# Prompt attention of branch A as one causal softmax per head, with branch counts in its bias table

## The reference

```python
# A: 8 heads of 64, branches (window, dilation) = (128,1), (512,4), (2048,16)
for window, dil in A_PATTERNS:      # keys i, i-dil, ..., i-window: up to 129 of them
    o, lse = banded_attn(qa, ka, va, rel_bias[:, :8], dil, window // dil, None)
oa = merge_branches(outs, lses)     # softmax over the three lse, weighted sum
# B: 8 query heads, 2 kv heads, window 128, a learned sink in each head's denominator
ob, _ = banded_attn(qb, kb, vb, rel_bias[:, 8:], 1, 128, sinks)
mixed = concat([oa, ob]); out = mixed @ w_out
```

## Time and profile before

| | |
|---|---|
| time of three runs, median (lowest to highest) | 2607.88 us (2606.56 to 2607.96) |
| the profiled execution | 2608.48 us, span 2606.7 us |
| TensorE busy | 90% |
| VectorE, ScalarE, GpSimd busy | 34%, 21%, 31% |
| granted TensorE clock, mean | 0.94 of full |
| prompt attention | 1264 to 1628 us |

### The profile page before, as it was taken

How to read it: one execution, slowest core, us unless ns; L and a number is a source line. 1 busy time by engine, 2 the same in 40 slices (tenths; PEclk the granted TensorE clock), 3 DMA queues, 4 the chain that set the end, 5 groups by cost and what they waited for, 6 DMA issues and landing times. The chain is left out here.

```text
span 2606.7 us, 37370 instructions
## 1 busy us (share of the span) xinstructions
PE 2350.6 (90%) x14418; PEld 2206.2 (85%) x14418; DVE 894.7 (34%) x2053; ACT 539.1 (21%) x781; POOL 810.4 (31%) x536
## 2 busy tenths in 40 slices
PE   4699999999999879995898776887999999999996
PEld 2599999999999779972677665876999999999995
DVE  0422222222222560024356776139222222222225
ACT  2111111111111212211233333122211111111114
POOL 1422322332222142132465443423323233232210
PEclk8899999999999989985999887998999999999998
DMA  8633323222110001136711000120111111111101
GB/s 263 216 100 97 97 80 97 87 61 77 49 49 25 17 20 45 48 91 170 178 34 34 18 17 25 40 73 1 49 48 48 48 48 48 45 39 44 40 1 65
DMA packets 211413, 171.56 MB, mean 66 GB/s; under 512 B 31847, under 2 KB 191703, under 8 KB 210840
## 3 DMA queue, kind: packets, MB, share of 16 engines
q1 hardware_dynamic: 211352, 170.76, 22.0%
HBM read 157.24 MB, written 19.26 MB: 68 GB/s over the span
## 5 line engine op out<-in xcount | busy, mean ns | idle before, releaser
L193 PE MATMUL psum<-Hhi,Whi 128*128 128x344 f32 x2736 | 881.0, 322 | 46.5 <-POOL Hlo L662 28.7
L195 PE MATMUL psum<-Hhi,Wlo 128*128 128x344 f32 x2736 | 878.2, 321 | 0.0
L194 PE MATMUL psum<-Hlo,Whi 128*128 128x344 f32 x2736 | 877.6, 321 | 0.0
L289 POOL TENSOR_TENSOR Wlo<-RAW,Whi 128x1024 fp32r<-128x1024 f32 x158 | 381.9, 2437 | 648.4 <-ACT Whi L285 647.7
L193 PEld LDWEIGHTS psum<-Hhi,Whi 128*128 128x128 f32 x2736 | 518.8, 190 | 49.8 <-issue 39.5
L195 PEld LDWEIGHTS psum<-Hhi,Wlo 128*128 128x128 f32 x2736 | 518.4, 189 | 0.0
L194 PEld LDWEIGHTS psum<-Hlo,Whi 128*128 128x128 f32 x2736 | 517.7, 189 | 0.2
L376 DVE TENSOR_TENSOR GF<-SIL,psum 128x344 f32<-128x344 f32 x132 | 67.6, 512 | 898.1 <-ACT SIL L358 898.1
L389 DVE SCALAR_TENSOR_TENSOR Y<-psum,G,Y 128x344 f32<-128x344 f32 (+1 forms) x528 | 302.6, 573 | 180.5 <-PE psum L195 180.5
L193 PE MATMUL psum<-Ghi,Whi 128*128 128x344 f32 x1056 | 339.8, 322 | 1.7 <-DVE yS L392 1.7
L194 PE MATMUL psum<-Glo,Whi 128*128 128x344 f32 x1056 | 338.2, 320 | 0.0
(11 more groups left out here) (196 smaller groups left out, 1816.8 us busy)
## 6 DMA issues: line engine op xcount, KB each, us to landing
ADA<-in_w_ada SPq DMA_DIRECT2D x36, 1024.0 KB, 8.9
RAW<-in_ffn_wg SPq DMA_DIRECT2D x44, 512.0 KB, 3.8
RAW<-in_ffn_wu SPq DMA_DIRECT2D x44, 512.0 KB, 3.8
RAW<-in_ffn_wd SPq DMA_DIRECT2D x44, 512.0 KB, 3.3
RAW<-in_w_in SPq DMA_DIRECT2D x18, 512.0 KB, 3.8
bias_rows<-bias_heads SPq DMA_DIRECT2D x4, 1536.0 KB, 15.4
SK<-in_cache_a_k SPq DMA_DIRECT2D x24, 256.0 KB, 3.3
SK<-in_cache_a_v SPq DMA_DIRECT2D x24, 256.0 KB, 4.3
```

What stands on the lines that cost most here:

```text
L193: pe.matmul(out, whi, xhi, start=first, stop=False)
L194: pe.matmul(out, whi, xlo, start=False, stop=False)
L195: return pe.matmul(out, wlo, xhi, start=False, stop=last)
L289: pool.tensor_tensor(Wlo[slot][:, :, :], RAW[raw][:, :, :], Whi[slot][:, :, :].bitcast(F32), ALU.subtract).then_inc(W[phase].ready, 1)
```

## The change

A becomes one softmax per head over all causal keys. The bias table of A holds, for each distance, the bias plus the logarithm of the number of branches that contain it, or a large negative number; `BIASA` has 1024 columns a head. The work is 40 units: 8 of B (one query block, all heads) and 32 of A (a pair of heads, one query block, all key blocks up to it). The scores of two heads are matmuls over 64 partitions, one on each half, into two banks. The reduction now gives the negated maximum, which ScalarE takes as its bias; ScalarE sums the exponentials too; GpSimd multiplies them by the reciprocal; then they are transposed and are the moving side of the value matmuls, whose output is already transposed, 64 partitions per head, 512 queries at a time. The masked queries, the column of ones, V16, V4, the records, the merge and the transposes of the mix are gone. All units are written out without loops. The query columns of B and the rows of w_out are fetched in another order so that the two kv heads lie on the two halves; the w_out fetch waits for the last transpose.

```diff
+EXTA = TP + P
+    for j in range(EXTA):
+        dist = TP - 1 - j
+        times = sum(0 <= dist <= P * step and dist % step == 0 for step in STEPS_OF[:3])
+        if times:
+            joint[t5_bucket(np.array(dist)), j] = 8.0
+            joint[32, j] = 8.0 * math.log(times)
+        else:
+            joint[32, j] = 8.0 * NEG
...
+        UNITS = 5 * TB
...
+        def scores_pe(pe, u, st):
...
+            if is_b(u):
+                n = (min(i, 1) + 1) * P
+                for t in (2 * st, 2 * st + 1):
+                    for e in range(2):
+                        h = slice(HD * e, HD * e + HD)
+                        last = pe.matmul(bank[2 * e + r][:, (t % 2) * 2 * P:(t % 2) * 2 * P + n],
+                                         projT[h, TQB + t, queries], projT[h, TKB, (i + 1) * P - n:(i + 1) * P],
+                                         start=True, stop=True)
             else:
+                t, first = u // TB - 1, 512 * st
+                n = min(512, (i + 1) * P - first)
+                for e in range(2):
+                    h = slice(HD * e, HD * e + HD)
+                    last = pe.matmul(bank[2 * e + r][:, 0:n], projT[h, TQA + t, queries],
+                                     projT[h, TKA + t, first:first + n], start=True, stop=True)
...
+                    last = dve.tensor_tensor_reduce(
+                        slot(u, e)[:, first:first + n], bank[2 * e + r][:, 0:n],
+                        BIASA[:, 2 * (u // TB - 1) + e, at:at + n], -SCALE, low if st else 3.0e38, ALU.add, ALU.min, low)
...
+                last = act.activation(s, s, ACT.Exp, bias=U_NEG[:, u % 3, e:e + 1], scale=-1.0,
+                                      accum_out=U_DEN[:, u % 3, e:e + 1])
...
+                    pool.tensor_scalar(s, s, U_RDEN[:, u % 3, e:e + 1], 1.0, ALU.mult, ALU.mult).then_inc(normed, 1)
...
+                for kb in range(4 * s + 4):
+                    lo = max(0, kb - 4 * s) * P
+                    for e in range(2):
+                        table = PTA0 if s == 0 else PTA1 if kb < 4 else PTA2
+                        last = pe.matmul(out[HD * e:HD * e + HD, lo:512], VT[:, kb, 2 * t + e, :],
+                                         table[:, e, kb % 4, lo:512], start=(kb == 0), stop=(kb == 4 * s + 3))
...
+        def attention_pe(pe):
...
+            for u in range(UNITS):
+                for half in range(2):
+                    scores_pe(pe, u + 2, half)
+                    turn_pe(pe, u, half)
+                values_pe(pe, u - 1)
+            values_pe(pe, UNITS - 1)
...
+        def attention_dve(dve):
...
+            for u in range(UNITS):
+                scores_dve(dve, u + 2, 0)
+                turn_evac(dve, u, 0)
+                scores_dve(dve, u + 2, 1)
+                recip_dve(dve, u + 1)
+                turn_evac(dve, u, 1)
+                outs_dve(dve, u - 1)
...
+            table_b_sp(sp)
             samp_tables_sp(sp)
             samp_values_sp(sp, 2)
             samp_new_sp(sp)
             samp_values_sp(sp, 0)
             samp_values_sp(sp, 1)
-            sp.wait_ge(v_stored, 16 * TB)
-            v16_sp(sp, range(0, 3))
+            table_a_sp(sp)
             for n in range(3, NS):
                 samp_values_sp(sp, n)
-                v16_sp(sp, range(n, n + 1))
-            b16_sp(sp)
-            v4_sp(sp)
-            late_tables_sp(sp)
+            sp.wait_ge(v_stored, 16 * TB)
             after_phase(sp, "wout")
-            pair_fetch(sp, "wout", wout_source, 0)
...
+            sp.wait_ge(t_done, PIECE_AT[UNITS])
+            with sp.Fori(0, KT // 2) as i:
+                wout_fetch(sp, i)
```

More of the change, by code:

```diff
@@ L743, in build @@
[L743 to L759, removed]
@@ L779, in build @@
         k_stored = [sem(f"k_stored{i}") for i in range(4)]
[L780 to L785, removed]
@@ L946, in scores_pe @@
-        def scores_pe(pe, hf):
-            if hf is None:
-                return
-            pe.wait_ge(q_staged, hf.x + 1)
-            pe.wait_ge(max_done, hf.x + 1)
-            if hf.is_b:
-                pe.wait_ge(b_in, 16 * 5)
-            n = hf.blocks * P
-            for j in range(4):
-                h = 4 * hf.hh + j
-                if hf.is_b:
-                    keys = projT[:, TKB, 0:TP] if h % 2 == h // 4 else kB2[:, :]
-                else:
-                    keys = projT[:, TKA + h // 2, 0:TP]
-                last = pe.matmul(bank[2 * hf.parity + j % 2][:, (j // 2) * 2 * P:(j // 2) * 2 * P + n],
-                                 qS[hf.slot][:, j, :], hf.columns(keys, True),
-                                 start=True, stop=True)
-            last.then_inc(qk_done, 1)
@@ L1027, in values_pe @@
-        def values_pe(pe, hf):
-            if hf is None:
-                return
-            pe.wait_ge(t_evac, hf.y + 2)
-            pe.wait_ge(o_evac, hf.x + 1)
-            nb = hf.blocks
-            for j in range(4):
-                for kb in range(nb):
-                    last = pe.matmul(bank[6 + hf.parity][:, j * AUG:(j + 1) * AUG], PTB[hf.parity][:, j, kb, :],
-                                     hf.values(4 * hf.hh + j, kb), start=(kb == 0), stop=(kb == nb - 1))
-            last.then_inc(pv_done, 1)
@@ new lines, in pieces @@
+        def pieces(u):
+            i = u % TB
+            if is_b(u):
+                return [(e, [kb]) for e in range(2) for kb in range(min(i, 1) + 1)]
+            return [(e, list(range(4 * c, min(4 * c + 4, i + 1)))) for e in range(2) for c in range(steps(u))]
+        STEP_AT = [sum(steps(v) for v in range(u)) for u in range(UNITS + 1)]
+        PIECE_AT = [sum(len(pieces(v)) for v in range(u)) for u in range(UNITS + 1)]
+        GROUP_END = list(range(TB)) + [TB + TB * t + 4 * s + 3 for t in range(4) for s in range(2)]
@@ new lines, in turn_pe @@
+        def turn_pe(pe, u, half):
+            for n, (e, kbs) in enumerate(pieces(u)):
+                if e != half:
+                    continue
+                p = PIECE_AT[u] + n
+                pe.wait_ge(normed, 2 * u + e + 1)
+                if p >= 2:
+                    pe.wait_ge(t_evac[p % 2], p // 2)
+                cols = [t * 2 * P + kbs[0] * P for t in range(4)] if is_b(u) else [kb * P for kb in kbs]
+                for j, c in enumerate(cols):
+                    last = pe.transpose(bank[4 + p % 2][:, j * P:(j + 1) * P], slot(u, e)[:, c:c + P], ident[:, :])
+                last.then_inc(t_done, 1)
@@ L1225, in kv_pe, with attention_pool @@
+        def attention_pool(pool):
+            for u in range(UNITS):
+                norm_unit_pool(pool, u)
         def kv_pe(pe, b):
@@ L1582, in _ @@
             after_phase(sp, "proj")
-            with sp.Fori(0, PT // 2) as i:
-                pair_fetch(sp, "proj", proj_source, i)
+            with sp.Fori(0, TQB // 2) as i:
+                proj_fetch(sp, i)
+            for t in range(4):
+                query_b_fetch(sp, t)
+            proj_fetch(sp, PT // 2 - 1)
             sp.wait_ge(proj_done, NG * PT)
```

713 lines of the change are left out of this document (264 added, 449 removed).

## The result

The changed kernel takes 2437.86 us (median of 4 runs, 2435.73 to 2439.11), the kernel before on the same chip 2607.92 (4 runs): a ratio of 0.9338, with an interval of 0.9324 to 0.9352. The direction was right, and so was the mechanism in the main (shorter chain, overlapping tiles); two steps of the sum for attention were not.

What follows compares the result with a forecast made beforehand. It took latency to bound the third attention stage. Attention 8 + 54 + 150 + 10 + 8 = 230 us, started at 1270.4 and followed by a 25 us tail, gained 123.6 on 2608.5: 2485 us, range 2447 to 2535.

Steps and rivals of the forecast that it cites:

- the tail: From attention's last output to the output projection's third column group: splits queued before TensorE starts it, 25 us with the PSUM copy.
- "4 us" for the B table: Sample stage: the 1 MB table goes out ahead of the sample tables, delaying the sample softmax 4 us, from 0 to 7.
- "2 us" for the A table: Sample stage: the 4.2 MB table goes ahead of sample values 3 to 7, small-piece copies go; 2 us, from -5 to 8.
- the fill: Start of attention: until the first unit is turned, eight reductions, eight exponentials and one product, 8 us.
- tile changes: Attention on TensorE: about 150 changes among three tile shapes at about 0.1 us, 15 us, of which 10 counted.
- A lone pair therefore takes 3 of 4 pass times: A's scores, one pair of matmuls per step, overlap only partly: 61.4 x 3/4 = 46.1 us.
- The adaLN row: Adaptive-norm projection, three 32-column tiles side by side: 24 matmuls take 3.58 us against 10.3 one after another.
- the loop's waits: TensorE waiting on other engines: B 6.7 us a unit against 5.9 of TensorE work; A 10 us a pair.
- block 6: A's query block 6: 3.6 us of reductions, reciprocal, normalizing and handoffs against some 1 us of TensorE work, about 2.6 lost.
- That nothing overlaps: Rival for attention: tiles give nothing, TensorE 218.5 us plus waits, fill, changes and clock, 286; total 2541 us, chance 0.05.
- That only the scores don't: Rival for attention: scores of two heads don't overlap, 252 us in place of 230; total 2507 us, chance 0.14.
- The low clock: Rival for attention: TensorE at 1.2 GHz all through, 374 us in place of 230; total 2629 us, chance 0.03.

Runs made afterwards that it cites:

- both score steps first: The changed kernel with both score steps of the unit two ahead placed before both transpose halves; 2431.4 us.
- the table last: The changed kernel with the load of A's bias table issued behind the last sample values instead of ahead of values 3 to 7; 2430.82 us.

## What the prediction had right, and which of its steps failed

The profiled execution ended 48.1 us ahead of the 2484.9 worked out. By landmarks: the start of attention 11.3, attention 34.5, the tail -0.3, behind it 2.6.

**The start: 1270.4 forecast, 1259.14 measured.** "4 us" for the B table: nothing; TensorE resumes after the sample softmax at 1221.24, before at 1221.39. "2 us" for the A table: its price is one wait of 2.43 us. But the copies of V16 that went had held up five sample loads, one by 0.52 and four by 1.15 to 1.45 us, and the last sample matmul ends 2.8 us earlier than before. From there to the first score matmul it took 3.0 us before and 0.5 now, another 2.5, counted nowhere: the masked queries had been staged there (GpSimd from 1262.87). The forecast knew that these copies go and took a range of -5 to 8; what it put at 4 + 2 was -5.3.

**Attention, B and A: 222 forecast, 185.5 measured.** The terms side by side:

| term | forecast | by the rows after | from |
|---|---|---|---|
| scores and values | 110.1 | 87.2 | 104,448 columns x 1.67 ns / 2 |
| transposes | 44.5 | 44.5 | 408 x 0.109 |
| waits | 49.4 | 20.6 | the rows of TensorE's waits, without the fill |
| tile changes | 10 | 22 to 30 | 150 x 0.15 to 0.2 |
| clock | 8 | about 9 | 0.90 over 49.5 us, 0.97 over 136 |

This column sums to 183 to 191; only the waits and the clock in it are read directly, the other terms are counts times prices. The step that failed first is "The two passes of a matmul follow each other on one tile. A lone pair therefore takes 3 of 4 pass times". A pair takes 2 pass times and the 0.2 us of a change. The adaLN row spoke against the step: if each matmul started a pass after the last, no number of tiles could overlap more than 2 deep, and there 2.9 of 3 did. The argument for three passes had no row. It cost 22.9 us. The second step that failed is the loop's waits, the largest error: 28.8 us. Of it 7.7 is the price of the product, 1.67 ns a column taken from a two-stream row where a one-stream product costs 0.84, under the lower bound of 1.0. The rest, about 21, is the model itself. It summed each unit's handoffs as if nothing else ran and charged the difference to TensorE, four blocks in each pair; yet scores two units ahead had been made by then, and a pair loses 3.2 us, the last 5.0, not 10. At block 6, forecast 2.6, one wait of 1.49 stands in the trace (1.91 in the last pair), elsewhere 0.29 to 0.53, and 0.83 before the last value run. The change price was undercounted, "15 us, of which I count 10": at 0.15 to 0.2 us each it is 22 to 30. This error made the forecast too short, the other two made it too long.

The Trainium skill (TensorEngine Tiling (Array Packing), Key Properties) has changes of the tiling mode drain the engine; the runs show a cost that fits, 0.15 to 0.2 us a change.

**The fill** was 10 us (1259.14 to 1269.1), forecast 8: the clock was 0.57 there.

**What held.** The tail, 25 forecast, 25.3 measured, by the queue on GpSimd that the forecast named. Bias matmuls and split fetches: nothing, with a wait of 8.9 us left before the first FFN. The value run, 5.8 and 5.74. No 1.7 us copies on VectorE. "GpSimd products of 1024 columns near 1.9 us" holds for B (1.895) and not for A (1.12).

**The rivals.** That nothing overlaps was priced at 2541 and, built, is 2518. That only the scores don't was priced 22 over the forecast; built, it is 43 over the changed kernel on one half of the rows and 18 on all rows. The low clock did not come: 0.90 in B and 0.97 in A, with transposes a quarter of TensorE's work. It was the right thing to fear, though: with both heads' scores on one half of the rows TensorE had 1.2 GHz for the first 46 us of attention.

## What to carry to other kernels

If a row shows that tiles overlap, price tiled matmuls at one over the number of tiles, and add every change of shape in full: net of them, the scores' overlap is worth 17.6 us here. Where a loop has work queued some units ahead, work its waits out from what TensorE still has to do, not from the sum of the handoffs, and before a slow engine's operation is priced by its cousin, ask how many streams each reads: here 1.67 and 0.84 ns a column, 8 us. In a tail, count what stands in one engine's queue: six subtractions moved to an idle VectorE gave 7.9 us of the tail, more than the 6.5 of a new order of the whole loop.

## What the runs showed of the hardware

Matmuls in float32 on two row halves, or two column halves, overlap in both passes; their first records start within 0.06 us of each other. A change between tiled and whole costs 0.15 to 0.2 us, in and out.

TensorE at 100% busy is not always at full clock: with all scores on rows 0 to 63 it was busy without a gap and was granted 0.51 for 46.5 us (1257.96 to 1304.50), then 1.00 with the same kinds of matmuls; with the values on one strip too, 0.50 for 34.3 us, then 1.00. The same matmuls on all 128 rows had 0.95 (1259 to 1269) and 0.96 (1269 to 1309), pairs on both halves 0.57 and 0.91. The first of these windows differs among kernels with pairs on both halves too, from 0.50 (both score steps first) to 0.78 (the table last). The Trainium skill (TensorE: Matmul & The Clock Gate, What's actually happening) has the clock follow how busy the engine has been; these 46.5 us at the lower level do not fit that, if busy is what the records show. What holds the level down is open. Transposes did no harm: they are a quarter of TensorE's work in A, and A was granted 0.97.

GpSimd's float32 product by a scalar of each row: 0.84 ns a column and 0.27 us. By a tensor that is broadcast: 1.67 and 0.18.
